# Prompt attention interleaved with the next group's q, k, v projections

## The reference

```python
ATT_GROUPS = ((128, 1), (512, 4), (2048, 16))  

def dilated_group_prompt(q, k, v, window, dil):
    b, s, h, e = q.shape
    blk = window // dil
...
    sc = jnp.einsum('bdnqhe,bdnkhe->bdnqhk', qb, kb, preferred_element_type=F32) * ATT_SCALE
...
    sc = jnp.where(valid[None, None, :, :, None, :], sc, -jnp.inf)
    lse = jax.nn.logsumexp(sc, axis=-1)
    pr = jnp.exp(sc - lse[..., None])
    o = jnp.einsum('bdnqhk,bdnkhe->bdnqhe', pr, vb.astype(F32))
...
def dilated_attention(xn, pos, bufs, wqkv, wo):
    b, t, _ = xn.shape
    qkv = (xn @ wqkv).reshape(b, t, 3, N_GROUPS, ATT_HEADS, ATT_HEAD_DIM)
    outs, lses, new = [], [], []
    for gi in range(N_GROUPS):
        window, dil = ATT_GROUPS[gi]
        q = rope(qkv[:, :, 0, gi], pos)
        k = rope(qkv[:, :, 1, gi], pos)
        v = qkv[:, :, 2, gi]
...
    wts = jax.nn.softmax(jnp.stack(lses), axis=0)
    o = jnp.sum(wts[..., None] * jnp.stack(outs), axis=0)
    y = o.reshape(b, t, ATT_WIDTH).astype(xn.dtype) @ wo
    return y, new
```

## Time and profile before

| | us |
|---|---|
| median of three runs | 4872.67 |
| lowest, highest | 4871.66, 4880.65 |
| the profiled execution | 4864.97 |
| its span, first to last instruction | 4863.2 |
| PE busy | 4493.0 (92%) |
| DVE busy | 1643.9 (34%) |
| ACT busy | 787.9 (16%) |
| mean granted clock of PE | 0.932 |

### The profile page before, as it was taken

One profiled execution on the slowest core, in us unless ns is written; L12 is line 12 of the kernel. 1 busy time (PEld: TensorE's weight loads), 2 busy tenths in 40 slices (PEclk: granted clock), 3 DMA queues, 4 the chain that ended last, 5 costly groups with the idle time before them and its releaser, 6 DMA issues. The chain is left out here.

```text
span 4863.2 us, 77445 instructions
## 1 busy us (share of the span) xinstructions
PE 4493.0 (92%) x34120; PEld 3076.8 (63%) x34120; DVE 1643.9 (34%) x2764; ACT 787.9 (16%) x1888; POOL 141.0 (3%) x143
## 2 busy tenths in 40 slices
PE   5999899999999999999979797979688899999998
PEld 2566778888756666665656464646477666666556
DVE  5000666666424333321122424343401343333101
ACT  1000222222112111111112121212100211111000
POOL 0000000000001000000000000000000100000001
PEclk8999899998899999999989898989756899999999
DMA  1111101000020111122320101010332011111223
GB/s 57 62 71 67 55 30 33 24 24 23 9 92 23 40 37 36 38 68 95 110 82 11 60 11 60 11 55 16 148 121 84 35 41 36 36 39 38 87 107 120
DMA packets 85332, 266.32 MB, mean 55 GB/s; under 512 B 37024, under 2 KB 43040, under 8 KB 76448
## 3 DMA queue, kind: packets, MB, share of 16 engines
q1 hardware_dynamic: 85024, 261.63, 15.3%
HBM read 226.01 MB, written 35.58 MB: 54 GB/s over the span
## 5 line engine op out<-in xcount | busy, mean ns | idle before, releaser
L279 PE MATMUL ps<-sb_h,sb_w 128*128 128x384 f32 (+1 forms) x4224 | 1289.8, 468 | 1.8 <-issue 1.8
L279 PEld LDWEIGHTS ps<-sb_h,sb_w 128*128 128x128 f32 x4224 | 801.7, 190 | 485.2 <-issue 2.8
L311 PE MATMUL ps<-sb_big,sb_w 128*128 128x384 f32 (+1 forms) x2112 | 646.6, 468 | 1.2 <-ACT sb_tmp L398 1.2
L311 PEld LDWEIGHTS ps<-sb_big,sb_w 128*128 128x128 f32 x2112 | 400.2, 190 | 241.6 <-ACT sb_tmp L398 2.2
L1429 PE MATMUL ps<-sb_h,sb_w 128*128 128x384 f32 (+1 forms) x960 | 303.0, 478 | 93.2 <-DVE sb_big L1616 80.7
L1429 PEld LDWEIGHTS ps<-sb_h,sb_w 128*128 128x128 f32 x960 | 185.6, 194 | 207.4 <-issue 88.9
L486 DVE COPY sb_tmp<-sb_tmp 128x2 f32<-128x2 f32 x88 | 14.9, 169 | 760.9 <-ACT sb_tmp L398 760.8
L1429 PE MATMUL ps<-sb_h,sb_tmp 128*128 128x384 f32 (+1 forms) x768 | 236.4, 469 | 0.0
L620 PE MATMUL ps<-sb_big,sb_w 128*128 128x384 f32 (+1 forms) x768 | 234.5, 468 | 0.0
L417 DVE TENSOR_TENSOR sb_tmp<-sb_tmp 128x384 f32<-128x384 f32 (+1 forms) x63 | 34.8, 552 | 526.8 <-ACT sb_tmp L343 525.0
L395 ACT ACTIVATE sb_tmp<-ps 128x384 f32<-128x384 f32 x176 | 86.4, 491 | 731.5 <-PE ps L279 731.5
(11 more groups left out here) (226 smaller groups left out, 4885.5 us busy)
## 6 DMA issues: line engine op xcount, KB each, us to landing
sb_w<-wdown SPq DMA_DIRECT2D x46, 1408.0 KB, 6.0
sb_w<-wup SPq DMA_DIRECT2D x88, 512.0 KB, 3.5
sb_big<-kT SPq DMA_DIRECT2D x8, 2304.0 KB, 11.4
sb_big<-vc SPq DMA_DIRECT2D x8, 2304.0 KB, 13.4
rkv_scratch<-sb_w SPq DMA_DIRECT2D x24, 544.0 KB, 2.7
sb_w<-wrkv SPq DMA_DIRECT2D x24, 512.0 KB, 3.5
sb_w<-wqkv SPq DMA_DIRECT2D x20, 512.0 KB, 6.5
sb_x<-xT SPq DMA_DIRECT2D x2, 4352.0 KB, 17.8
```

The source lines that it names most:

```text
L279: mm = pe.matmul(m.ps[:, 3 * q + b, 0:n], wt[f % 2][q][:, k, :], m.H[:, k, t0:t0 + n], start=(k == 0), stop=(k == KT - 1))
L311: mm = pe.matmul(m.ps[:, u % 6, 0:n], wdt[u % 2][:, f, :], hid[:, f, t0:t0 + n], start=(f == 0), stop=(f == FT - 1))
```

## The change

Only `prompt_attention` changes. The hardware loops are written out. The twelve slots form one sequence; while slot s has its attention blocks computed, the projections of slot s+1 are computed too.

- The work of a projection is divided into 17 pieces: three blocks each of q, k and v (`Q`, `K`, `V`), three rotations each of q and k (`rQ`, `rK`), and two halves of v's transposes (`T`). `STEPS` says which pieces go into which of the ten steps of the slot before. In a step PE does `scores(n)`, the first half of the step's product (channels 0 to 3), `turn(n-1)`, the second half and the rotation or the transposes, and `values(n-2)`. Slot 0's pieces are done ahead, with nothing between.
- All pieces share a ring of two PSUM banks (0 and 1): a piece waits until the piece two before it has been taken, by ACT for products and transposes and by DVE for rotations. Scores keep two pairs of banks; turned blocks have one bank instead of two, and so have values.
- In `scores` the order of the loops is turned round: the key block is outside, the head inside.
- q and k have two tiles each, v and `Vt` one. Three weight buffers instead of nine: the next slot's weight is fetched when the last block of its kind has been computed. At the start three weights are fetched ahead of the constants instead of nine behind them.
- The merge of a round is cut into ten steps and done by DVE in the ten steps of the next round's group 0, between bias and rotation; group 0's `NMZ` has two tiles for that. ACT takes the merge's exponentials in steps 2 to 4. The last round's merge follows the last slot.
- q of group 2 is sorted by stride in the last addition of the rotation; the separate copy goes.

The diff, cut:

```diff
--- before.py
+++ after.py
@@ -1343,278 +1343,360 @@
...
+    SLOTS = [(i, g) for i in range(AP_) for g in range(3)]
+    NSLOT = len(SLOTS)
+    STEPS = [[("Q", 0)], [("Q", 1)], [("Q", 2), ("rQ", 0)], [("K", 0), ("rQ", 1)], [("K", 1), ("rQ", 2)], [("K", 2), ("rK", 0)],
+             [("V", 0), ("rK", 1)], [("V", 1), ("rK", 2)], [("V", 2)], [("T", 0), ("T", 1)]]
+    PIECES = [(s, p) for s in range(NSLOT) for step in STEPS for p in step]
+    NUMBER = {p: n for n, p in enumerate(PIECES)}
+    TAKEN, counts = {}, {"a": 0, "d": 0}
+    for s, p in PIECES:
+        who = "d" if p[0] in ("rQ", "rK") else "a"
+        counts[who] += 1
+        TAKEN[s, p] = (who, counts[who])
...
-        wl = [sem(f"wl{n}") for n in range(9)]
-        bt = lambda n, c=1: m.big[:, n * T:(n + c) * T]
-        Q, K, V, R = bt(0), bt(1), bt(2), bt(3)
-        NMZ = [tiles(m.big, (4 + 3 * g) * T, 3, T) for g in range(3)]
+        diff, wexp = sem("diff"), sem("weight_exp")
+        wl = [sem(f"wl{n}") for n in range(3)]
+        Q, K, V, R, QP, COS, SIN = [bt(0), bt(4)], [bt(1), bt(5)], bt(2), bt(3), bt(6)[:, 0:SEQ], bt(20), bt(21)
+        rows = {"Q": Q, "K": K, "V": [V, V]}
+        NMZ0 = [tiles(m.big, 7 * T, 3, T), tiles(m.tmp, 0, 3, SEQ)]
+        NMZ12 = [tiles(m.big, 10 * T, 3, T), tiles(m.big, 17 * T, 3, T)]
...
+        wt = [tiles(m.w, n * D, KT, P) for n in range(3)]
+        SM = [m.w[:, 3 * D + s * 1024:3 * D + s * 1024 + 512].rearrange("p (h k) -> p h k", h=2) for s in range(2)]
+        PT = [m.w[:, 3 * D + s * 1024 + 512:3 * D + s * 1024 + 1024].rearrange("p (h k q) -> p h k q", h=2, k=2) for s in range(2)]
...
+        def ring(s, p):
+            return NUMBER[s, p] % 2
+        def wait_piece(eng, s, p):
+            eng.wait_ge(proj, NUMBER[s, p] + 1)
+        def wait_taken(eng, s, p):
+            who, count = TAKEN[s, p]
+            eng.wait_ge(pta if who == "a" else ptd, count)
...
+            for t in range(3):
+                weights(0, t)
+            for t, n in ((rot, "c_rot"), (SIN, "c_sin"), (COS, "c_cos"), (masks, "c_amask")):
                 sp.dma_start(t, a[n]).then_inc(consts, 16)
-            with sp.Fori(0, AP_) as i:
...
+            for s, (i, g) in enumerate(SLOTS):
+                for t, n in enumerate("QKV"):
+                    if s + 1 < NSLOT:
+                        wait_piece(sp, s, (n, 2))
+                        weights(s + 1, t)
+                    if n == "V":
+                        sp.wait_ge(roped, 2 * s + 2)
+                        wait_taken(sp, s, ("V", 2))
+                        for k, src in enumerate((Q[s % 2], K[s % 2], V)):
+                            sp.dma_start(scratch[k, i + g * 4], src[:, SEQ:T]).then_inc(kvst, 16)
+                        sp.dma_start(a["o_k"][i + g * 4], K[s % 2]).then_inc(kvst, 16)
+                        sp.dma_start(a["o_v"][i + g * 4], V).then_inc(kvst, 16)
+            sp.wait_ge(kvst, 16 * 5 * NSLOT)
...
+            def product(s, p, ks):
+                n, b = p
+                t = "QKV".index(n)
+                t0, w = TB[b]
+                if ks[0] == 0:
+                    pe.wait_ge(wl[t], 16 * (s + 1))
+                    if NUMBER[s, p] >= 2:
+                        wait_taken(pe, *PIECES[NUMBER[s, p] - 2])
+                for k in ks:
+                    mm = pe.matmul(m.ps[:, ring(s, p), 0:w], wt[t][:, k, :], m.H[:, k, t0:t0 + w], start=(k == 0), stop=(k == KT - 1))
+                if ks[-1] == KT - 1:
+                    mm.then_inc(proj, 1)
+            def rotate(s, p):
+                n, b = p[0][1], p[1]
+                t0, w = TB[b]
+                wait_taken(pe, s, (n, b))
+                wait_taken(pe, *PIECES[NUMBER[s, p] - 2])
+                pe.matmul(m.ps[:, ring(s, p), 0:w], rot, rows[n][s % 2][:, t0:t0 + w], start=True, stop=True).then_inc(proj, 1)
...
+            def advance(s, n, part):
+                if s >= NSLOT:
+                    return
+                for p in STEPS[n]:
+                    if p[0] in ("Q", "K", "V"):
+                        product(s, p, range(4 * part, 4 * part + 4))
+                    elif part and p[0] == "T":
+                        transposes(s, p)
+                    elif part:
+                        rotate(s, p)
...
+                for q, kt in ((0, before(g, n)), (1, n)):
+                    for h in range(2):
...
+            for n in range(10):
+                advance(0, n, 0)
+                advance(0, n, 1)
+            for s in range(NSLOT):
+                for n in range(10):
+                    if n < 8:
+                        scores(s, n)
+                    advance(s + 1, n, 0)
+                    if 1 <= n <= 8:
+                        turn(s, n - 1)
+                    advance(s + 1, n, 1)
+                    if n >= 2:
+                        values(s, n - 2)
...
+            def take_piece(s, p):
+                n, b = p
+                wait_piece(act, s, p)
+                if n == "T":
+                    if s:
+                        act.wait_ge(nfull, 8 * s)
+                    act.activation(Vt[:, 4 * b:4 * b + 4, :].rearrange("p n j -> p (n j)"), m.ps[:, ring(s, p), :],
+                                   ACT.Copy).then_inc(pta, 1)
+                    return
+                if p == ("V", 0) and s:
+                    act.wait_ge(kvst, 80 * s)
+                t0, w = TB[b]
+                act.activation(rows[n][s % 2][:, t0:t0 + w], m.ps[:, ring(s, p), 0:w], ACT.Copy).then_inc(pta, 1)
...
+            for s, (i, g) in enumerate(SLOTS):
+                for n in range(10):
+                    if n < 8:
+                        exps(s, n)
+                    if 1 <= n <= 8:
+                        take_turned(s, n - 1)
+                    if g == 0 and i and n in (2, 3, 4):
+                        weight(i - 1, n - 2)
+                    if s + 1 < NSLOT:
+                        for p in STEPS[n]:
+                            if p[0] in ("Q", "K", "V", "T"):
+                                take_piece(s + 1, p)
+            for g in range(3):
+                weight(AP_ - 1, g)
...
+            def turned(s, p):
+                n, b = p[0][1], p[1]
+                t0, w = TB[b]
+                t = rows[n][s % 2]
+                wait_piece(dve, s, p)
+                dve.tensor_tensor(R[:, t0:t0 + w], m.ps[:, ring(s, p), 0:w], SIN[:, t0:t0 + w], ALU.mult).then_inc(ptd, 1)
+                if b < 2:
+                    return
+                dve.tensor_tensor(t, t, COS, ALU.mult)
+                dve.drain()
+                if SLOTS[s][1] == 2 and n == "Q":
+                    apart = lambda ap: ap[:, 0:SEQ].rearrange("p (j r) -> p r j", r=16)
+                    dve.tensor_tensor(QP.rearrange("p (r j) -> p r j", r=16), apart(t), apart(R), ALU.add)
+                    dve.tensor_tensor(t[:, SEQ:T], t[:, SEQ:T], R[:, SEQ:T], ALU.add).then_inc(roped, 1)
+                else:
+                    dve.tensor_tensor(t, t, R, ALU.add).then_inc(roped, 1)
+                dve.drain()
...
+            def merge(i, n):
+                N, M, Z = ([nmz(i, g)[:, c, 0:SEQ] for g in range(3)] for c in range(3))
+                low = QP
+                if n == 0:
+                    dve.drain()
+                    dve.tensor_tensor(low, M[0], M[1], ALU.min)
+                    dve.drain()
+                    dve.tensor_tensor(low, low, M[2], ALU.min)
+                if n == 1:
+                    dve.drain()
+                    for g in range(3):
+                        dve.tensor_tensor(M[g], low, M[g], ALU.subtract).then_inc(diff, 1)
+                if n in (3, 4, 5):
+                    dve.wait_ge(wexp, 3 * i + n - 2)
+                    dve.tensor_tensor(N[n - 3], N[n - 3], M[n - 3], ALU.mult)
+                    dve.tensor_tensor(Z[n - 3], Z[n - 3], M[n - 3], ALU.mult)
+                if n in (6, 7):
+                    dve.drain()
+                    dve.tensor_tensor(Z[0], Z[0], Z[n - 5], ALU.add)
+                    dve.tensor_tensor(N[0], N[0], N[n - 5], ALU.add)
+                if n == 8:
+                    dve.drain()
+                    dve.reciprocal(Z[1], Z[0])
+                if n == 9:
+                    dve.drain()
+                    dve.tensor_tensor(AO[:, i, 0:SEQ], N[0], Z[1], ALU.mult)
...
+            for s, (i, g) in enumerate(SLOTS):
+                for n in range(10):
+                    if n < 8:
+                        bias(s, n)
+                    if g == 0 and i:
+                        merge(i - 1, n)
+                    if s + 1 < NSLOT:
+                        for p in STEPS[n]:
+                            if p[0] in ("rQ", "rK"):
+                                turned(s + 1, p)
+                    if n >= 2:
+                        take_values(s, n - 2)
+            for n in range(10):
+                merge(AP_ - 1, n)
```

(60 more changed lines are left out.)

281 lines of the change are left out of this document (65 added, 216 removed).

## The result

| | before | after |
|---|---|---|
| median, us | 4876.7 (4 runs) | 4733.6 (4 runs) |
| span of the profiled execution | 4863.2 | 4740.6 |
| prompt attention, first DMA issue to the next stage's first read | 989.1 | 859.2 |
| DVE and ACT busy in the whole span | 1643.9, 787.9 | 1644.7, 788.9 |

What follows compares the result with a forecast made beforehand. The stage was taken as a chain, with PE nearest to full but waiting; start, first slot, woven slots, bare last slot and last merge summed to 858.3, say 859 us against 988.9, giving 4743 us, range 4703 to 4806.

Steps and rivals of the forecast that it cites:

- first DMA to first product: Stage start: the first product waits for its weight, with three weights now ahead of the constants; 8.4 becomes 9.4 us.
- first slot's dense work and transposes: First slot, with nothing to weave with: its dense work stays bare, 50.3 + 0.5 + 1.0 = 51.8 us.
- eleven woven slots: Slots with attention blocks between dense work: 525.8 us dense, 186.5 blocks, 16.6 transposes, 7 + 3 + 11 for losses.
- last slot's blocks: Last slot's attention blocks stay bare: 18.9 us, perhaps 1.5 more with one bank instead of two, 20.4 us.
- last merge: After the last slot: the last round's merge stays as it is, 26.8 us.
- The cuts: Products cut in halves around the transposes: 0.07 us lost per visit, 96 visits, 7 us.
- the first rival: Every array-shape change beside a dense matmul exposes it: 33 to 70 us given back, 4770 to 4806 us; chance 0.17.
- The one buffer of transposed values: End of each slot: the next q product waits for ACT's copy of transposed values, 0.3 us per slot, 3 us.
- The reciprocal: Merging slots, step 8: it holds DVE, the copy of values 6 queues behind, values 7 wait 3.6 us; 11 us.
- second rival: Slots with a merge stretch by all of it, 81 us back instead of 11: saving 60, 4813 us; chance 0.05.
- third rival, slower: Circle of rotation, bias, exponentials, eviction and product longer than a step: 3.3 us exposed per step, +160, 5033 us; chance 0.05.
- the forecast's slack: Woven step: scores behind a delayed bias are needed as exponentials only later, leaving about 4 us, so DVE costs nothing there.

Runs made afterwards that it cites:

- later reciprocal: Changed kernel with each merge's reciprocal in four quarters in steps 2 to 5 of the group 1 slot and its last multiplication in step 6: stage 847.7 us.
- The load experiments: Changed kernel with three or six spare 512-column DVE multiplications behind the bias in each of 110 woven steps: stage 867.2 and 943.1 us.

## Why the prediction was right

The forecast was 4743 us, with a range of 4703 to 4806; the median is 4733.6. The stage was to take 859 us and takes 859.2.

**The sum, term by term.** In the changed kernel the stage begins at 2508.65 us. Its first product and the wait before it, and the bare last slot, its first scores and its last values:

```profile
2518.71 16.71 PE L1454 MATMUL ps<-sb_h,sb_w 128*128 128x384 f32 x48 [14.14 <-DMA sb_tmp<-c_amask]
```

```profile
3320.72 1.12 PE L1502 MATMUL ps<-sb_big 64*128 64x128 f32 x8
...
3340.31 0.64 PE L1536 MATMUL ps<-sb_ident,sb_tmp 128*64 128x128 f32 x8
```

| term | forecast | measured |
|---|---|---|
| first DMA to first product | 9.4 | 10.1 |
| first slot's dense work and transposes | 51.8 | 52.9 |
| eleven woven slots | 749.9 | 749.2 |
| last slot's blocks, to 3340.95 | 20.4 | 20.2 |
| last merge, to 3367.84 | 26.8 | 26.9 |
| sum | 858.3 | 859.2 |

**The woven slots.** The forecast was 525.8 dense, 186.5 blocks, 16.6 transposes, 7 for cuts, 3 for the one buffer of transposed values, 11 for the reciprocal. Without a merge the eleven slots take 736.2 us (their sum in that kernel), where my terms without the last give 738.9: 3 us too much. This is a balance of two errors. With the 7 us for cuts, of which nothing is there, taken out, the other terms give 731.9, 4.3 us too little. A full step of group 0 should have been 5.16 + 0.65 + 2.32 = 8.13 us and is 8.11. The method, taking a block's cost from the weight loads of the earlier trace rows with 0.17 at each border, carried the sum.

**The cuts (forecast 7, measured 0)** were sized from the six small matmuls of the earlier trace rows. The same step with the product whole takes the same 8.11 us. The 0.07 us per visit lay within the reading of the rows: 29.52 us over 96 instructions, a third of them of 320 columns, is 0.3256 us for one of 384 and not 0.3225, which leaves 0.02. (In the woven step eight of them take 2.58 us from start to start, 2617.75 to 2620.33, which is 0.3225 each.) The visits are 88 (eight steps of eleven slots have both a product and transposes), not 96.

**Borders of shape beside dense work (the first rival).** In the step above the values come 0.74 us after the rotation starts, 2620.33 to 2621.07, where the rotation's own two matmuls take 0.65: 0.09 us per step, at most 10 us over all 110 steps, and not 33 to 70. The whole step says the same: 8.11 us less 5.81 of dense matmuls leave 2.30 for the block with all its borders, where the earlier trace rows gave 2.32. With the rule that a change of mode drains TensorE (the Trainium skill, "TensorEngine Tiling (Array Packing)", section "Tiling Modes") these rows agree as far as a price goes, 0.09 us behind 384 columns here and 0.17 us of the weight loader in the earlier trace rows; they don't show the drain itself. The rival falls.

**The one buffer of transposed values (forecast 0.3 per slot)** is there: PE waits six times, 1.9 us in all, and the slots behind group 2's are 67.1 instead of 66.7 us.

**The reciprocal (forecast 3.6 us in three slots).** PE's timeline around the last values of two merging slots, and DVE's around the first:

```profile
2836.16 1.23 PE L1473 MATMUL ps<-sb_ident,sb_big 128*128 128x128 f32 x8
2840.18 0.69 PE L1529 MATMUL ps<-sb_w,sb_tmp 128*64 128x128 f32 x4 [2.79 <-DVE sb_tmp L1651]
...
2842.99 7.22 PE L1454 MATMUL ps<-sb_h,sb_w 128*128 128x384 f32 x16
...
3250.53 0.44 PE L1529 MATMUL ps<-sb_w,sb_tmp 128*64 128x128 f32 x4 [2.79 <-DVE sb_tmp L1651]
...
3252.47 5.40 PE L1454 MATMUL ps<-sb_h,sb_w 128*128 128x384 f32 x16
```

```profile
2829.28 0.49 DVE L1618 TENSOR_TENSOR sb_big<-ps,sb_big 128x320 f32<-128x320 f32 x1 [2.46 <-PE ps L1463]
2829.68 1.28 DVE L1621 TENSOR_TENSOR sb_big<-sb_big 128x1088 f32<-128x1088 f32 x1
2831.04 1.29 DVE L1628 TENSOR_TENSOR sb_big<-sb_big 128x1088 f32<-128x1088 f32 x1
2832.43 0.56 DVE L1651 COPY sb_tmp<-ps 128x384 f32<-128x384 f32 x1
2833.07 6.55 DVE L1676 RECIPROCAL sb_big<-sb_big 128x1024 f32<-128x1024 f32 x1
2839.54 0.49 DVE L1651 COPY sb_tmp<-ps 128x384 f32<-128x384 f32 x1
```

The wait is 2.79 us, three times, and DVE's part is as told: the reciprocal holds it from 2833.07 to 2839.62 and the copy of values 6 stands behind it. The last rotation was 1.2 us earlier than I reckoned (2832.33, 2.1 us into step 8, not 3.3), because DVE even waited 2.46 us for PE's rotation. What I had left out is the clock: behind two of these waits the next sixteen dense matmuls take 7.22 us and 7.09, behind the third 5.40. So the term is 13.0 us (the sum of slots with the merge, 749.2, less that without, 736.2) instead of 11. Each of the three waits was 0.8 us too long in the forecast, and the clock was left out; the net, 2 us too little, stands against the 3 us too much above. That the sum came within 1 us is partly luck.

**The merge on the path (second rival)** falls in the strict form: with a later reciprocal, nothing of it is left on PE. In one piece, it costs 39.3 us of the 130 (898.5 against 859.2).

**No weaving (third rival, slower)** falls: in a woven slot no product ever waited for ACT's eviction of a product, and the six short waits above are all that PE saw of ACT there. The load experiments put its threshold between 2.2 and 4.5 us of added DVE work per step, the forecast's slack being 4.

**Where the 130 us come from.** From 989.1 to 898.5 by weaving with the merge in one piece (and all else in the change but the spreading), 90.7 us; from 898.5 to 859.2 by spreading the merge, 39.3. Without any merge weaving is worth 896.6 - 823.0 = 73.6 us, 12 more than I expected ahead of those runs, since the kernel before keeps pauses of 3.6 to 3.9 us, where I had 1.5, and its slow starts behind them. Writing the loops out gives nothing with the merge and 1.8 us without it. In the kernel before part of a block's time is lower clock and not waiting (last section); no run separates the two in the 90.7 us.

**What stays open.** The whole time fell by 143 us in the median, 13 more than the stage. The interval of the ratio is 28 us wide, and the stretches before and behind the stage drift by more than 13. In the nine other runs of woven kernels the median fell by between 8 us less and 18 us more than the stage did in the profile. So nothing here says whether some of it is the change's.

## What to carry to other kernels

When PE waits for small chains, weaving independent dense work between their steps left just their matmuls here: cost it as weight loads plus a fixed price per change of array shape, and sum engine by engine through one step. Spread a serial stage on another engine in pieces no longer than the step's slack, and look at the longest single instruction first: here one reciprocal of 6.55 us was the only part of the merge that PE still saw. Put what can come late (a division, a final multiplication) into a slot where that engine has slack.

## What the runs showed of the hardware

Short pauses of PE cost clock. Behind two of the three pauses of 2.79 us, themselves behind a stretch of small matmuls, the next sixteen dense matmuls ran partly at the lower of the two levels (1.2 GHz): 7.22 and 7.09 us at a granted clock of 0.75 and 0.76, against 5.40 at 1.00 behind the third. Behind the three pauses of 2.22 us (before, written out, no merge) the q and k products took 31.2 us instead of 29.5. The loss is 1.7 to 1.8 us each time. Without these pauses (reciprocal later) the eleven woven slots ran at a granted clock of 1.00 throughout.

Blocks of small matmuls with still shorter waits ran at the lower level too. In the kernel before, the blocks of group 1 and of group 2 in the second round, with no wait of PE over 1.5 us in them (columns as in the earlier trace rows):

```profile
2862.00:2888.50 26.50, 22.50 (x194) 17.07 (x192) 14.50 (x23) 12.54 (x43) 0.00 (x0) 0.87 0.06 23
2936.00:2958.00 22.00, 18.46 (x168) 12.44 (x168) 10.75 (x22) 10.94 (x43) 0.00 (x0) 0.84 0.66 243
```

At 0.87 and 0.84 some 7 us of each stretch are at the lower level, which by estimate costs up to 3.5 us. So weaving gained clock besides filling waits; the forecast costed the blocks at the high clock and so took this for granted.

The turn of a hardware loop with this body can delay PE. From DVE's end to PE's first matmul it is 1.66 us with the loop and 0.05 without, and PE stood idle for 3.94 us in all at the turn: the turn takes at least some 1.6 us and at most 3.9. The Trainium skill, "Runtime: NRT & Kernel Launch", section "Instruction fetch mechanics", says that a taken branch whose target lies outside the pages at hand breaks the sequential prefetch of instructions and stalls; the runs agree in direction, and don't show the fetch itself.
